# Forgetting attention with two matmuls where there were three, and another order of each step's work on ACT and DVE

## The reference, cut to what matters

```python
def fox_attention(q, k, v, c):        # 16 heads of 64, 1024 positions
    ...
    s = jnp.einsum('bhqd,bhkd->bhqk', qb, k).astype(jnp.float32) * scale
    s = s + (cb[..., :, None] - c[..., None, :])
    s = jnp.where(kpos[None, :] <= qpos[:, None], s, -jnp.inf)
    w = jax.nn.softmax(s, axis=-1)
    return jnp.einsum('bhqk,bhkd->bhqd', w.astype(v.dtype), v)

def fox_mixer(u, w_in, b_f, w_out):
    ...
    log_f = jax.nn.log_sigmoid(fl + b_f)
    c = jnp.cumsum(log_f, axis=1).transpose(0, 2, 1)
    attn = fox_attention(heads(q), heads(k), heads(v), c)
    return (attn * jax.nn.silu(g)) @ w_out
```

## Time and profile before

| | |
|---|---|
| time before, median of 3 runs | 3930.71 us (3926.98 to 3938.69) |
| the profiled execution: its own time, and its span | 3930.58 us, 3928.6 us |
| PE busy (matmuls), share of the span | 3640.7 us, 93% |
| PEld busy | 2996.8 us, 76% |
| DVE busy | 2038.1 us, 52% |
| ACT busy | 1672.7 us, 43% |
| POOL busy | 108.0 us, 3% |
| granted clock of PE, mean | 0.951 of full speed |
| the chain of work that ended last | PE 35%, DVE 5%, ACT 4% of the span as its named parts |

### The profile page before, as it was taken

The page is one execution under the profiler, slowest core; times in us unless marked ns, Lnnn a source line. Parts: engine busy times, 40 slices in busy tenths (PEclk is TensorE's granted clock), DMA queues, the critical chain, the costliest instruction groups (busy, mean ns, idle before and its releaser), DMA issues. The chain is left out here.

```text
span 3928.6 us, 48656 instructions
## 1 busy us (share of the span) xinstructions
PE 3640.7 (93%) x19058; PEld 2996.8 (76%) x19058; DVE 2038.1 (52%) x3959; ACT 1672.7 (43%) x3118; POOL 108.0 (3%) x119
## 2 busy tenths in 40 slices
PE   7999889999997999899897999999869999999799
PEld 6888558778876777777786877777758888888687
DVE  3144443453345677776335455555555456666552
ACT  3222561454442344443225444444443466665431
POOL 0011220000000000000000000000000000000000
PEclk9999999999997788989999999999979999999899
DMA  4343412113222211222311101010032121110321
GB/s 143 115 134 105 141 40 89 58 68 108 95 74 82 57 44 44 56 53 65 134 38 63 28 28 33 28 28 28 27 108 81 54 65 38 44 38 17 121 78 43
DMA packets 219339, 264.59 MB, mean 67 GB/s; under 512 B 62700, under 2 KB 142692, under 8 KB 218088
## 3 DMA queue, kind: packets, MB, share of 16 engines
q1 hardware_dynamic: 219112, 261.48, 20.6%
HBM read 191.43 MB, written 69.99 MB: 67 GB/s over the span
## 5 line engine op out<-in xcount | busy, mean ns | idle before, releaser
L332 PE MATMUL bank<-wh,XH 128*128 128x512 f32 x1344 | 536.3, 399 | 24.1 <-DVE wl L316 19.0
L332 PE MATMUL bank<-wh,XL 128*128 128x512 f32 x1344 | 529.1, 394 | 0.0
L332 PE MATMUL bank<-wl,XH 128*128 128x512 f32 x1344 | 528.5, 393 | 0.0
L2633 PE MATMUL bank<-XH,wh 128*128 128x512 f32 x1040 | 426.0, 410 | 28.2 <-DVE wl L2622 26.7
L2633 PE MATMUL bank<-XH,wl 128*128 128x512 f32 x1040 | 410.5, 395 | 0.0
L2633 PE MATMUL bank<-XL,wh 128*128 128x512 f32 x1040 | 409.6, 394 | 0.0
L332 PEld LDWEIGHTS bank<-wh,XH 128*128 128x128 f32 x1344 | 256.5, 191 | 77.9 <-DVE wl L316 12.6
L332 PEld LDWEIGHTS bank<-wl,XH 128*128 128x128 f32 x1344 | 255.8, 190 | 54.1
L332 PEld LDWEIGHTS bank<-wh,XL 128*128 128x128 f32 x1344 | 256.4, 191 | 51.0
L332 PE MATMUL bank<-XH,wh 128*128 128x512 f32 x704 | 280.8, 399 | 8.0 <-DVE XL L1585 8.0
L316 DVE TENSOR_TENSOR wl<-raw,wh 128x1024 fp32r<-128x1024 f32 x128 | 157.1, 1237 | 250.8 <-ACT wh L307 249.3
(11 more groups left out here) (419 smaller groups left out, 7155.0 us busy)
## 6 DMA issues: line engine op xcount, KB each, us to landing
sc_zt<-stage SPq DMA_DIRECT2D x88, 256.0 KB, 2.0
raw<-in_att_w_in SPq DMA_DIRECT2D x33, 512.0 KB, 4.1
raw<-in_even_w_in SPq DMA_DIRECT2D x32, 512.0 KB, 4.9
raw<-in_odd_w_in SPq DMA_DIRECT2D x32, 512.0 KB, 4.5
raw<-in_rec_w_in SPq DMA_DIRECT2D x32, 512.0 KB, 4.0
sc_h<-H SPq DMA_DIRECT2D x24, 512.0 KB, 2.6
sc_z<-stage SPq DMA_DIRECT2D x40, 256.0 KB, 2.0
z<-sc_z SPq DMA_DIRECT2D x8, 1024.0 KB, 5.8
```

What stands on the lines that cost most here:

```text
L332: done = e.matmul(out, lhsT, rhs, start=k == 0 and j == 0, stop=k == NK - 1 and j == 2)
L2633: done = e.matmul(bank[:, :], x[:, k, :], y[:, k, ts], start=k == 0 and j == 0, stop=k == NK - 1 and j == 2)
```

## The change

- **Scores, two matmuls.** The operand tiles `qh, ql, kh, kl` become `qq, kk, qx, kx`. `qq` has qh in the head's own 64 rows and ql in the other 64; `kk` has kh in both. qq·kk is therefore qh·kh + ql·kh. `qx` has qh and, in the other rows, the sums and ones; `kx` has kl and the same: qx·kx is qh·kl and the forgetting term. For this, ACT copies each of q and k twice (L2922 becomes two lines), and DVE's low part goes to other rows. At the start only two of four tiles have to be zeroed.
- **Values, two matmuls.** `vh` and `vl` become one tile `vv` with, for each key block, the columns high of the even head, low of it, low of the odd head, high of it. The stationary operand is the high and low part of one head, 128 columns. It is multiplied by WH and by WL; the high part's rows and the low part's rows of bank 5 have to be added afterwards. That is new work: `rest` (ACT copies the 64 low rows, 256 columns) and `mixed` (DVE adds them to the high rows, then multiplies by the gate and by 0.5).
- **Gate.** sigmoid(g) is computed as (tanh(g/2) + 1) / 2: ACT's tanh with scale 0.5, DVE's "+1, times g", and the 0.5 in `mixed`.
- **Order.** `low` of n-2 in place of n-3, both parts after `normed`; `rest` and `mixed` one step after the matmuls (n-5, at even n); the splits at s = 2, 6, 10, 14 in place of 3, 7, 11, 14. The store of a finished pair and ACT's copy of the last pair hang on `mixed`, and so move with it.

```diff
-SPLITS = ("qh", "ql", "kh", "kl")
+SPLITS = ("qq", "kk", "qx", "kx")
...
-        order += [("low", n - 3, 0)] * at(3) + [("turned", n - 2)] * at(2) + [("exps", n)] * at(0)
-        order += [("low", n - 3, 1)] * at(3) + [("normed", n - 1)] * at(1)
+        order += [("rest", n - 5)] * (at(5) and n % 2 == 0) + [("turned", n - 2)] * at(2) + [("exps", n)] * at(0)
+        order += [("normed", n - 1)] * at(1) + [("low", n - 2, half) for half in range(2)] * at(2)
+        order += [("mixed", n - 5)] * (at(5) and n % 2 == 0)
...
-            long |= {3: ("split", i + 1), 7: ("split", i + 2), 11: ("split", i + 3), 14: ("split", i + 4),
-                     8: ("load", 2 * p, "rows"), 9: ("load", 2 * p, "q"), 10: ("load", 2 * p, "k")}
+            long |= {8: ("load", 2 * p, "rows"), 9: ("load", 2 * p, "q"), 10: ("load", 2 * p, "k")}
...
+        if p < 8 and s % 4 == 2 and number[p, "q"] + s // 4 + 1 < len(seq):
+            order.append(("split", number[p, "q"] + s // 4 + 1))
...
-            for j, (u, v) in enumerate((("qh", "kh"), ("ql", "kh"), ("qh", "kl"))):
+            for j, (u, v) in enumerate((("qq", "kk"), ("qx", "kx"))):
...
-            for j, (v, w) in enumerate(((vh, self.WH), (vl, self.WH), (vh, self.WL))):
-                done = e.matmul(bank[:, off:256], v[:, ks], w[x][:, kb, off:256], start=kb == top and j == 0,
-                                stop=kb == 0 and j == 2, skip_group_check=True)
+            for j, w in enumerate((self.WH, self.WL)):
+                done = e.matmul(bank[:, off:256], v[:, kb, :], w[x][:, kb, off:256], start=kb == top and j == 0,
+                                stop=kb == 0 and j == 1, skip_group_check=True)
...
-                e.activation(self.x[n % 2][name + "h"][hr, :], self.raw[name][hr, :], ACT.Copy, scale=0.125 if name == "q" else 1.0) \
-                    .then_inc(*self.high.up(n, name))
+                scale, x, src = 0.125 if name == "q" else 1.0, self.x[n % 2], self.raw[name][hr, :]
+                e.activation(x[2 * name][hr, :], src, ACT.Copy, scale=scale).then_inc(*self.high.up("own", n, name))
+                second = x["qx"][hr, :] if name == "q" else x["kk"][self.other_rows(n), :]
+                e.activation(second, src, ACT.Copy, scale=scale).then_inc(*self.high.up(n, name))
...
+            if what == "rest":
+                h, x = n // 8, n // 2 % 2
+                e.wait_ge(*self.weighted.at(n))
+                if n >= 4:
+                    e.wait_ge(*self.mixed.at(n - 4))
+                e.activation(self.rest[x][self.rows_of(h)[0], :], c.banks[5][self.other_rows(h), 0:256], ACT.Copy).then_inc(*self.lower.up(n))
...
-            e.activation(self.half(self.g[p % 2], half), bank[:, :], ACT.Sigmoid).then_inc(*self.copied.up(p, name, half))
+            e.activation(self.half(self.g[p % 2], half), bank[:, :], ACT.Tanh, scale=0.5).then_inc(*self.copied.up(p, name, half))
...
-            for n in SPLITS:
+            for n in SPLITS[2:]:
...
-        e.wait_ge(*self.weighted.at(n))
+        e.wait_ge(*self.lower.at(n))
+        e.tensor_tensor(rest, self.c.banks[5][hr, 0:256], rest, ALU.add).then_inc(*self.mixed.up("sum", n))
+        e.wait_ge(*self.mixed.at("sum", n))
...
-        e.tensor_tensor(g, self.c.banks[5][hr, 0:256], g, ALU.mult).then_inc(*self.mixed.up(n))
+        e.scalar_tensor_tensor(out=g, in0=rest, scalar=0.5, in1=g, op0=ALU.mult, op1=ALU.mult).then_inc(*self.mixed.up(n))
```

More of the change, by code:

```diff
@@ L2686, in fox_order @@
         if p < 8:
-            i = number[p, "q"]
-            long |= {3: ("split", i + 1), 7: ("split", i + 2), 11: ("split", i + 3), 14: ("split", i + 4),
-                     8: ("load", 2 * p, "rows"), 9: ("load", 2 * p, "q"), 10: ("load", 2 * p, "k")}
-        if n < 128 and s in long and not (long[s][0] == "split" and long[s][1] >= len(seq)):
+            long |= {8: ("load", 2 * p, "rows"), 9: ("load", 2 * p, "q"), 10: ("load", 2 * p, "k")}
+        if n < 128 and s in long:
             order.append(long[s])
+        if p < 8 and s % 4 == 2 and number[p, "q"] + s // 4 + 1 < len(seq):
+            order.append(("split", number[p, "q"] + s // 4 + 1))
         if p == 8 and 4 <= s < 11:
             order.append(("back", s - 4))
+    order += [("rest", 127), ("mixed", 127)]
     return seq, order
@@ L2732, in __init__ @@
         self.scored, self.turned, self.vturned, self.weighted = (c.flag("pe") for _ in range(4))
-        self.copied, self.high, self.expd, self.whigh, self.vhigh, self.xhigh, self.biased, self.logged = (c.flag("ac") for _ in range(8))
+        self.copied, self.high, self.expd, self.whigh, self.vhigh, self.xhigh, self.biased, self.logged, self.lower = (
+            c.flag("ac") for _ in range(9))
         self.ready, self.zeroed, self.low, self.most, self.scale, self.wlow, self.vlow, self.gated, self.mixed, self.summed = (
@@ L2752, in rows_of, with other_rows, v_bank, v_high @@
         return slice(64 * (h % 2), 64 * (h % 2) + 64), 64 * (1 - h % 2)
+    def other_rows(self, h):
+        return slice(64 * (1 - h % 2), 64 * (1 - h % 2) + 64)
+    def v_bank(self, p, half):
+        return self.c.banks[self.mms[p, "v'", half]][:, :].rearrange("p (k a e) -> p k a e", k=4, a=2)
+    def v_high(self, p, half):
+        return self.v[p % 2][:, 4 * half:4 * half + 4, 0:4:3, :]
+    def v_low(self, p, half):
+        return self.v[p % 2][:, 4 * half:4 * half + 4, 1:3, :]
     def half(self, t, half):
@@ L2789, in sp @@
                 self.sp_rows(e, n)
-            elif what == "weighted" and n % 16 == 15 and n < 112:
+            elif what == "mixed" and n % 16 == 15 and n < 112:
                 p = n // 16
@@ L2806, in sp_rows @@
             e.wait_ge(*self.scored.at(8 * (h - 2) + 7))
[L2807 removed]
+        for dst, r, j in (("qx", 2, 0), ("qx", 3, 1), ("kx", 0, 2), ("kx", 1, 3)):
             e.dma_start(f32(self.x[h % 2][dst][at + r:at + r + 1, :]), self.zt[2048 + 16 * j + h:2049 + 16 * j + h, :]) \
@@ L2872, in pe_scores @@
             bank, kc = self.c.banks[self.sb[n, part]], slice(512 * part, 512 * part + w)
-            for j, (u, v) in enumerate((("qh", "kh"), ("ql", "kh"), ("qh", "kl"))):
+            for j, (u, v) in enumerate((("qq", "kk"), ("qx", "kx"))):
                 if j == 1 and part == half:
                     e.matmul(bank[:, w - P:w], self.idr[:, :], self.negr[:, :], start=False, stop=False, skip_group_check=True)
-                done = e.matmul(bank[:, 0:w], x[u][:, qs], x[v][:, kc], start=j == 0, stop=j == 2)
+                done = e.matmul(bank[:, 0:w], x[u][:, qs], x[v][:, kc], start=j == 0, stop=j == 1)
             done.then_inc(*self.scored.up(n) if part == half else self.scored.up(n, 0))
@@ L2911, in ac @@
                     e.wait_ge(*self.weighted.at(16 * (n - 2) + 15))
-                e.activation(self.half(self.vh[n % 2], half), c.banks[self.mms[n, "v'", half]][:, :], ACT.Copy) \
-                    .then_inc(*self.vhigh.up(n, half))
+                e.activation(self.v_high(n, half), self.v_bank(n, half), ACT.Copy).then_inc(*self.vhigh.up(n, half))
             elif what == "load" and rest[0] != "rows":
@@ L2952, in ac @@
                 e.activation(c.XH[:, n, :], self.back_row(n), ACT.Copy).then_inc(*self.xhigh.up(n, 1))
-            if what == "weighted" and n >= 112 and n % 4 == 3:
+            if what == "rest":
[4 more added lines that the diff above has]
+                e.activation(self.rest[x][self.rows_of(h)[0], :], c.banks[5][self.other_rows(h), 0:256], ACT.Copy).then_inc(*self.lower.up(n))
+            if what == "mixed" and n >= 112 and n % 4 == 3:
                 hr, half = self.rows_of(n // 8)[0], n % 8 // 4
@@ L3029, in ve @@
                                     f32(self.WH[x][:, kbs[0]:kbs[-1] + 1, qs]), ALU.subtract).then_inc(*self.wlow.up(n, g))
-            elif what == "weighted":
-                self.ve_weighted(e, n)
+            elif what == "mixed":
+                self.ve_mixed(e, n)
             elif what == "back":
```

26 lines of the change are left out of this document (14 added, 12 removed).

## The result

The changed kernel takes **3792.45 us** (median of 4 runs, 3777.73 to 3805.68) against 3928.85 us for the kernel before (median of 4, 3925.83 to 3938.69). The ratio is **0.965, with a 95% interval of 0.961 to 0.969**: 136 us less. 88 us less had been forecast, 3843 us, with a range from 3817 to 3895. The direction was right, the time lies outside the range, and the gain is half as large again as forecast.

The account below looks back on a forecast made before the run. PE's queue was taken to bound the middle stages. Matmuls and waits give 55 + 13 us in six stages, 7.5 + 1.5 in the first; last stage 9, start 2.4, less 0.8: 88 off 3930.6, 3843 us; range 3817 to 3895.

Parts of the forecast that it names:

- What bounds the kernel, and the matmuls: Middle stages: PE's own queue is the clock; dropped matmuls, priced by distance between starts, save 9.2 us a stage.
- What the new order does to PE's waits: Attention stages: 4.3 us of waits could go, 2.2 taken; 13 us for six stages, 1.5 in the first.
- The half that was given back: Middle stages: half of 4.3 us not counted, for PE's shorter steps and DVE's `low` waiting in the same step.
- The bound: PE's waits in a middle stage: at best all 4.3 us gone, or at worst 4.2 us more.
- The last stage: A chain through three engines sets its time; 11 us off, 2 on, 9 in all; bounds 21 less, 5 more.
- The ends: Start: four zeroing casts fall, 2.4 us less; end: one more ACT copy and DVE instruction, 0.8 us more.
- Rival 1: Whole attention: only the matmuls go, waits don't shrink, last stage gains nothing; 65 us less, 3866 us; chance 0.25.
- Rival 2: Attention stages: ACT's double copies of q and k reach PE, 4.2 us a stage; 3895 us; chance 0.17.
- Rival 3: Attention stages: shorter PE work opens gaps, an eighth runs at half clock; 3933 us, no change; chance 0.03.
- Rival 4: Two-part steps: PE waits 1.9 us each for transposes, ACT's copy and DVE's `low`; 3972 us; chance 0.04.
- Rival 5: PE: the third matmul is not where its time goes, as weight loads run beside; chance folded into Rival 1.
- ACT's tables: Gate tiles on ACT: four loads of 1.28 us a stage go, 5.1 us; by the skill's price 10.8 us.

Follow-up runs that it names:

- e3: Changed kernel with as many matmuls as before added back (480 for 416 in a stage): middle stage 82.1 us against 73.4.
- e2: Kernel before, three matmuls per product, with only the changed order, tanh and new splits: middle stage 82.0 us against 91.5.
- e4: Changed kernel with only the low parts put back (block n-3, one before the maximum, one behind): middle stage 80.9 us against 73.4.
- e5: Changed kernel with only the gate's work put back into the step of its value matmuls: middle stage 78.6 us against 73.4.
- e7: Changed kernel with the weight splits back at s = 3, 7, 11, 14: middle stage 78.6 us against 73.4.
- e8: Changed kernel with a third ACT copy of q and of k at each load: middle stage 76.1 us against 73.4.
- e9: Changed kernel with SP's loads of pairs 0 to 2 issued before its wait for pair 6: last stage 76.8 us against 83.8.
- e1: Two matmuls in the whole order of the kernel before, with sigmoid and old splits: middle stage 96.1 us against 91.5 before; 3960.5 us.
- e10: e1 without the low rows' copy on ACT and sum on DVE (output incomplete): middle stage 84.9 us against 96.1.
- e6: Changed kernel with sigmoid in place of tanh, so four table loads a stage again: middle stage 74.6 us against 73.4.

## Why the prediction was right or wrong

**What bounds the kernel, and the matmuls: right.** PE's queue sets the middle stages, and each matmul is worth its distance from start to start. 9.2 us of a stage were forecast, 8.7 (`e3`) and 8.6 (`e2` to the change) measured. New instructions on DVE and ACT were priced right to 0.01 us each, and in this order they cost nothing there.

**"What the new order does to PE's waits": this step failed.** It took 2.2 us a stage, 13 for the six, by giving back half of the 4.3 us that could go. `e2` measured 9.5 us a stage, 57 for the six. What was wrong in it:
- The half that was given back. The reasons were PE's shorter steps and `low` waiting in the same step for PE's transposes and ACT's copy. `low` does wait, 5.0 us of a stage, but PE doesn't wait behind it: 0.2 us of PE's idle time is left.
- The bound, and not only the choice inside it. It counted only rows that the order named and left 0.8 us for v's copy and half of the split's wait standing, as though they had causes of their own. Nearly all of the 6.5 us went.
- The price of a wait: it costs more than its idle time. The six stages before have 549.2 - 511.5 = 37.7 us in which PE is idle. The same matmuls without waits take 492.2 us (`e2`), 57.0 less. So another 19.3 us, 3.2 a stage, were lost beside the waits. The part of it that rows explain is the clock. The chain of before shows, behind two waits of 0.98 and 0.88 us for `WL`, six projection matmuls in 2.56 us that elsewhere take 1.39:

```profile
2361.20 0.44 PE bank L2854 x2
2361.64 2.56 PE bank L2633 x6
...
2368.93 1.39 PE bank L2633 x6
```

and the granted clock in the two places is 0.50 and 1.00, the lower and the upper level:

```profile
2361.64:2364.20 2.56, 2.56 (x9) 1.99 (x7) 0.49 (x1) 2.50 (x6) 0.00 (x0) 0.50 0.33 97
2368.93:2370.32 1.39, 1.39 (x8) 1.13 (x8) 1.05 (x2) 1.37 (x3) 0.00 (x0) 1.00 0.00 0
```

The six stages before have four such stretches at 0.50 to 0.51, at 2361.5, 2453.6, 2545.8 and 2730.1 us, together 13.6 us long. By an estimate from the two rows, where the lower level makes the work about twice as long, they cost about 7 of the 19.3 us. The other 12 us, 0.2 us for each of some 58 waits, are what remains of the difference; they were not taken apart. What a wait costs beside its idle time is no fixed share: the six stages are longer than the same work without waits by 1.5 times PE's idle time before and in `e4`, by 1.7 times in `e5`, but by 1.2 times in `e7` and `e8`. `e7` has one stretch at the lower level in its six stages, `e8` none.

The terms also don't add up freely. From before, the order gives 9.5 us of a stage and the matmuls then 8.6, and these two do add up to the 18.1 measured. Taken first, the matmuls lose 4.6 us, and the order then gives 22.7.

The forecast was 50 us short over the attention (138 against 88). The six stages and the first make 46 of them (108.9 against 68, 14.5 against 9). All of that is in this step, since the matmuls were priced a little too high. The last stage makes 5, and the ends go 1 the other way.

**The last stage:** 13.7 us against 9, inside the bounds of 5 more to 21 less. The mechanism was as described, down to the first `back` copy, which was to wait 5 us or more and waited 6.1. `e9` prices that: 7 us of the stage go when the loads come earlier. The forecast started from a stage of 93.6 us, which was a block short by the border set right above.

**The ends:** from the zeroing to the first block 1.0 us was gained (62.6 to 61.6), not 2.4.

**Rivals.** Rival 1, only the matmuls go: no. In the changed kernel PE's waits went too, and with the matmuls' part of the change alone (`e1`) the kernel was slower than before instead of 65 us faster. Rival 2, ACT's double copies reach PE: no, but `e8` shows that it was close, with 2.7 of the next 4.2 us arriving. Rival 3, the clock: the opposite happened. The middle stages run at 1.00, the full 2.4 GHz; the lower level appears where the old order makes waits, with a mean of 0.95 in `e1`. The Trainium skill, page "TensorE: Matmul & The Clock Gate", section "HAM oscillation", has the rule that gaps bring PE to half clock. The trace agrees in that the lower level stands behind waits, but not behind each: there were four such stretches for some 58 waits before, and none in `e8`, where PE's waits are 15 us in six stages. Here the rule spoke for the change and not against it. Rival 4, the same-step chain: it does not bite where it was placed. DVE's low part waits 5 us of a stage for ACT's copy, and nobody waits for DVE. A chain of just that kind, with the low rows' copy as its link, is what made `e1` slower, as `e10` shows. Rival 5: refuted by `e3`.

**ACT's tables:** a load is 1.28 us in the trace, and nothing else stands around it: before, ACT's last read ends at 2349.81 us, the load runs from 2349.83 and the sigmoid starts at 2351.12. The Trainium skill, page "ScalarE: Activation LUTs", section "Table sets: the hidden batching unit", has about 2.7 us for it. That tanh and exp share a set, as the same section has it, is borne out, since no load is left in the stages. `e6` gives 1.2 us of a stage for the four.

## What to carry to other kernels

Where one engine has its waits scattered in a long stream, take as the bound of a reordering the whole of its idle time and what it loses beside it. That is what the stream takes now, less its length at its best distances from start to start. New small instructions on engines that have much room can cost more than they are long, if they stand inside a step's chain rather than a step behind. Removing work from the bounding engine also shortens the time in which the others must deliver; here that was 2 us of a stage at most, and not separated from the second copies. Test the order and the removal of work apart, since neither measures the other.

## What the runs showed that had not been expected

- The middle stages took 440.3 us in all four profiled executions of the changed kernel and of its version with earlier loads, with PE busy throughout. The spread of the times comes from elsewhere: the attention alone began between 2172.0 and 2199.9 us.
- In the last stage, some 77 matmuls more (`e3`) left the length as it was, 84.3 for 83.8 us, while the mean clock rose from 0.76 to 0.86 and PE's idle time fell. The matmuls cost time and the clock gave some back; that the length came out the same does not show that either is free:

```profile
2709.00:2792.80 83.80, 50.61 (x261) 42.67 (x259) 61.80 (x139) 44.85 (x103) 0.00 (x0) 0.76 0.21 70
2760.90:2845.20 84.30, 56.76 (x338) 49.23 (x336) 61.80 (x139) 44.60 (x102) 0.00 (x0) 0.86 0.21 69
```

- `e2` has the last stage at 76.1 us with the same wait for the DMA as the changed kernel, 5.5 us against 6.1. What it lacks is the low rows' copy and sum and the second copies, and its mean clock is 0.89 in place of 0.76. Which of these make the 8 us was not tried.
